# A two-layer hybrid decoder step with the order of every engine's steps written out as tables

## The chip, the cores and the metric

The kernel runs on one core of one Trainium2 chip. The metric is device time in microseconds (us), as the median of the runs. Six places matter: TensorE (PE), VectorE (DVE), ScalarE (ACT), GpSimd (POOL), SyncE (SP, which here only issues transfers), and the DMA engines that carry them out. Each engine works through its own list of instructions in order, and waits where an operand isn't ready.

## The reference

Two layers of one decoder block, over 1024 new tokens of a prompt and 8 × 4 tokens of running samples, in float32. The reference, cut to its core:

```python
def mixer_layer(x, pos, S0, k_past, v_past, buf, n_past, norm_pre, w_in, ret_gn_w, sb_bias, ...):
    h = rmsnorm(x, norm_pre)
    p = h @ w_in
    rq, rk, rv, rg, sq, sk, sv, sg, ca, cb, cg = jnp.split(p, idx, axis=-1)
    o_r, S = retention(rope(rq), rope(rk) * HEAD_DIM ** -0.5, rv, S0)
    o_r = head_groupnorm(o_r, ret_gn_w) * jax.nn.silu(rg)
    o_s = stickbreak(sq, k_all, v_all, sb_bias, n_past) * jax.nn.silu(sg)
    o_c, buf_new = conv_module(ca, cb, buf, dw_w, dw_b, ln_w, ln_b, pw_w)
    o_c = o_c * jax.nn.silu(cg)
    y = jnp.concatenate([o_r, o_s, o_c], axis=-1) @ w_out
    return x + rmsnorm(y, norm_post), S, sk_h, sv_h, buf_new
```

The model is 1024 wide, has 6 retention heads and 6 stick-breaking heads of 64, and a causal convolution over 31 tokens in 256 channels. In stick-breaking attention a score z gives log_stop = log sigmoid(−z), and its weight is exp(log sigmoid(z) + the sum of log_stop over all keys between it and the query), so every block of keys needs the totals of the blocks behind it.

## The kernel before

The 1056 tokens lie along the free axis, in 3 chunks of 352 (c = 0, 1, 2). What each engine does is cut into named **steps**, and each engine's program is a loop over a list of such steps that opens a branch for each kind. A step's instructions and its semaphore waits are the same wherever it stands in the list.

- **proj.i.c**: column block i of a weight matrix times chunk c. A layer has 54 blocks: 30 of the input projection, then 24 of the output projection, whose 8 column blocks come once for each chunk. A step has 24 matmuls of 128 rows × 352 columns. Each weight and each activation is split into a high and a low part, so eight row blocks take three products each: high·high (L1199), weight high · activation low (L1200), weight low · activation high (L1201). The result goes to one of three PSUM banks used in turn (`ring`). `claim` (L1171) makes PE wait until the bank's former job has been copied out by ACT (`proj` on ACT, L1611 among others).
- **wload.i** (L1447, a DMA issued by ACT), **whi.i** (ACT, L1459) and **wlo.i** (DVE or POOL, L1049) bring a block's weights in and split them.
- **sqx** (ACT, L1488), **sum_x** (PE, L1426), **nrm** (DVE, L1796), **hi** (ACT, L1580) and **lo** (L1040) make the normed, split activations of a chunk: squares, their sum, scaling, high and low part.
- Retention works on pairs of heads (p = 0 to 5, three in each layer). **swap** (SP, L1121) and **rot** rotate queries and keys, **glu_rest** (SP, L1087 and L1088) stores the convolution's state, **dec** (POOL, L2057 and L2061) applies the decay, **vtok** (PE, L1212) turns values over, **att.p.n** (PE, L1222 and L1224) and **ro.p.n** (PE, L1241, L1249, L1256) make block n of 128 tokens, and **gn_mean** (PE, L1278) and **gn_var** the group norm.
- Stick-breaking attention works on the same pairs, in 12 units u of a key block and a run of queries. Unit u goes through **score** (PE L1323, then ACT exp L1528, POOL L2101), **log** (ACT L1536, DVE L1770), **halve** (ACT L1550, DVE L1777), **stop** (PE L1337 and L1339, then ACT L1709) and **weigh** (PE totals L1353 and L1354, ACT L1719, PE product with the values L1359). `halve` of unit u on ACT waits for the totals of `weigh` of unit u − 1, which read the same buffers.
- The convolution (**taps** on DVE L1916, its norm **ln_mean** on PE L1290), and for the sample tokens **sample_k**, **sample_v** and **sample_o** on PE, with exp on ACT at L1743.
- The end of a layer: **root_y** (L1183), **post** (DVE L2042), **res** (L1031), and the stores of the result from SP: **store.l.c.h** (L1163), two for each chunk and four for the last chunk. **oldx** (SP, L1155) brings the residual back, **pages** (SP, L1059) copies 16 pages of the key or value cache.

Most matmuls use the whole array, 128 rows by 128 columns of weights. Some don't, and hold two or four small ones at a time: `score` 64 × 128, the value product of `weigh` 128 × 64, `ro` 64 × 64 and 128 × 64, `sum_x`, `sample_k` and `sample_v` 128 × 32. The profile prints this **form** beside the operation (as 64*128).

What sets the order is a planner, run when the kernel is built. `plan` (L532 to L706) names every step with a guessed duration and the steps that it needs; `RANKS` and `TURNS` hold numbers that push a kind of step, or one step, forward or back; `Plan.order` then replays the whole program: at each turn it picks, over all engines, the ready step with the lowest start time plus penalty. On PE it adds 0.09 where a step begins in another form than the last one ended. Five lists come out: 702 steps for PE, 1118 for ACT, 853 for DVE, 246 for POOL and 91 for SP.

Of the kernel before, what the change touches and what calls it, by code (L numbers as in the profile page):

```python
# [141 lines left out]
GATES = [("cb", 0), ("cb", 1), ("rg", 0), ("sg", 0), ("ln_act", 1), ("ln_act", 0), ("sg", 1), ("rg", 1), ("cg", 0), ("cg", 1), ("rg", 2), ("sg", 2)]  # L142
LATE = [("gn", 0), ("ln", 0), ("gn", 1), ("gn", 2)]
# [51 lines left out]
def helper(q):  # L195
# [3 lines left out]
SHARED_BY_DVE = ("taps", "taps9", "halve", "join", "rot", "gated", "wlo", "lo", "splo", "res", "glu_rest", "ln_act", "ln_var", "gn_var")  # L199
SHARED_BY_POOL = ("wlo", "rot", "dec", "own", "lo", "splo", "res")  # L200


RANKS = {("DVE", "log"): 2, ("PE", "ro"): -5, ("PE", "all_x"): -26, ("DVE", "sample_l"): 3, ("ACT", "root_x"): 2, ("SP",
         "glu_rest"): 296, ("SP", "pages"): 51, ("POOL", "res"): -11, ("DVE", "ln_act"): 12, ("SP", "oldx"): 239.5, ("SP",
         "swap"): 29.5, ("POOL", "own"): 9, ("SP", "store"): 147.5, ("ACT", "ln_act"): 6, ("SP", "stout"): 97, ("ACT", "gn_var"):
         2.5, ("PE", "sum_x"): -34, ("PE", "sample_o"): 21.5, ("DVE", "att"): 2.5, ("POOL", "rot"): 0.5, ("DVE", "halve"): 1,
         ("PE", "proj"): 4.5, ("POOL", "dec"): -3, ("PE", "vtok"): -42, ("DVE", "glu_rest"): 13.5, ("ACT", "wload"): 1, ("SP",
         "vout"): 125.5, ("PE", "weigh"): -4.5, ("POOL", "wlo"): 1, ("DVE", "post"): -9, ("DVE", "ln_var"): 1, ("PE", "stop"):
         -3.5, ("ACT", "att"): -7.5, ("PE", "att"): -5.5, ("DVE", "rot"): 2, ("ACT", "score"): 0.5, ("DVE", "q9"): 13, ("ACT",
         "proj"): 0.5, ("DVE", "taps"): 0.5, ("PE", "score"): 1.5, ("DVE", "res"): -8.5, ("ACT", "sample_l"): 2.5, ("DVE",  # L210
         "sample_o"): 6, ("ACT", "ro"): -7.5, ("PE", "gn_var"): 5, ("PE", "pw"): -51, ("ACT", "sigmoid"): -1, ("DVE", "st"): 0.5,
         ("POOL", "score"): -1.5, ("ACT", "halve"): 0.5, ("ACT", "pw"): -4.5, ("DVE", "ln_mean"): 1.5, ("SP", "pwload"): 212,
         ("ACT", "log"): -1, ("ACT", "k9"): 8, ("PE", "sample_v"): -76.5, ("DVE", "gn_mean"): 0.5, ("ACT", "root_y"): 1.5,
         ("ACT", "sample_k"): -1, ("ACT", "hi"): -2, ("ACT", "part"): 1, ("ACT", "gn_mean"): 1.5, ("ACT", "weigh"): -0.5, ("DVE",
         "wlo"): -0.5, ("DVE", "join"): 0.5, ("DVE", "proj"): 0.5}
# [59 lines left out]
class Plan:


    def __init__(self):
# [11 lines left out]
    def order(self):  # L290
# [18 lines left out]
        while left:  # L309
            best = None  # L310
            for n, t in ready.items():
                e, step = n
                if e == "PE" and step[0] in ring_kinds:
# [8 lines left out]
                    if t is None:  # L322
                        continue
# [1873 lines left out]
```

## Time and profile before

| | us |
|---|---|
| median of 3 runs | 1347.22 (1347.12 to 1348.54) |
| the profiled execution, span | 1346.0 |
| PE busy in it | 1317.3 (98%) |
| DVE busy | 834.3 (62%) |
| ACT busy | 772.9 (57%) |
| POOL busy | 464.9 (35%) |

The span is the time from the first to the last instruction of the profiled execution, which was one run of the same program as the timed ones. Matmuls of one stream overlap in the records: each is shown with 0.32 us and the next begins 0.16 us later. So the time that a stretch on PE costs is read from the starts of its rows, and not from their durations.

### The profile page before, as it was taken

What the parts mean: (1) busy time and instruction counts of PE and PEld (TensorE: products, weight loads), DVE (VectorE), ACT (ScalarE), POOL (GpSimd) and SP (SyncE); (2) the same over time, 40 slices, a digit from 0 to 9 for tenths busy, and PEclk for the clock granted to TensorE, in tenths of its full rate; (3) what the DMA queues carried; (4) which work ended last, traced back from release to release, by engine and by line L of the source; (5) the groups of instructions that cost most, each with busy time, mean ns of one, the idle gap of its engine ahead of it and who ended that gap; (6) DMA issues with size and microseconds to landing.
All of it is one profiled execution on the core that took longest, in us unless ns stands there. A gap on an engine that the chain in (4) does not pass through costs nothing.

```text
span 1346.0 us, 23077 instructions
## 1 busy us (share of the span) xinstructions
PE 1317.3 (98%) x8532; PEld 1136.4 (84%) x8532; DVE 834.3 (62%) x1306; ACT 772.9 (57%) x1535; POOL 464.9 (35%) x418
## 2 busy tenths in 40 slices
PE   6999999999999999999999999999999999999996
PEld 4988788887788887899998888888879788789996
DVE  4447787986542446466773587889764245554665
ACT  6464554655564666575655555456575456667552
POOL 2424532344422444141243345324343423423111
PEclk9999999999999999999999999999999999999998
DMA  7301103212024100275343120131101321006453
GB/s 251 113 22 57 38 32 91 81 46 60 17 69 132 56 19 30 73 237 171 109 139 123 43 57 32 57 113 44 47 26 54 80 83 48 33 10 226 154 184 118
DMA packets 92242, 113.61 MB, mean 84 GB/s; under 512 B 30818, under 2 KB 75618, under 8 KB 92002
## 3 DMA queue, kind: packets, MB, share of 16 engines
q1 hardware_dynamic: 76866, 56.56, 14.0%
q10 hardware_dynamic: 15264, 55.58, 12.8%
q8 instruction: 68, 1.11, 0.4%
q14 instruction: 44, 0.36, 0.1%
HBM read 88.15 MB, written 17.46 MB: 78 GB/s over the span
## 4 chain that ended last, share of the span: by engine, by line
PE 94%; ACT 2%; DVE 1%; POOL 1%; issue 1%; DMA 0%; SPq 0%; ACTq 0%; DVEq 0%; POOLq 0%
PE ring L1199 23%; PE ring L1201 21%; PE ring L1200 21%; PE Z L1323 4%; PE AV L1359 4%; PE Z L1337 2%; PE Z L1339 2%; PE ring L1278 2%; PE ring L1222 2%; PE Z L1353 2%; PE Z L1354 1%; PE ring L1241 1%; PE ring L1301 1%; PE ring L1237 1%; PE ring L1290 1%
## 5 line engine op out<-in xcount | busy, mean ns | idle before, releaser
L1199 PE MATMUL ring<-H_hi,w_hi 128*128 128x352 f32 x1776 | 594.3, 335 | 5.7 <-DVE H_lo L1040 4.9
L1201 PE MATMUL ring<-H_hi,w_lo 128*128 128x352 f32 x1776 | 572.3, 322 | 0.0
L1200 PE MATMUL ring<-H_lo,w_hi 128*128 128x352 f32 x1776 | 571.1, 322 | 0.0
L1199 PEld LDWEIGHTS ring<-H_hi,w_hi 128*128 128x128 f32 x1776 | 334.1, 188 | 43.2 <-issue 30.8
L1200 PEld LDWEIGHTS ring<-H_lo,w_hi 128*128 128x128 f32 x1776 | 335.1, 189 | 4.5
L1201 PEld LDWEIGHTS ring<-H_hi,w_lo 128*128 128x128 f32 x1776 | 334.4, 188 | 0.0
L2101 POOL TENSOR_SCALAR attend<-attend 128x512 f32<-128x512 f32 (+4 forms) x144 | 188.9, 1328 | 319.4 <-ACT attend L1528 319.3
L1916 DVE SCALAR_TENSOR_TENSOR MX<-MX,vec_sb 128x1023 f32<-128x1023 f32 (+14 forms) x120 | 166.7, 1389 | 2.2
L1770 DVE SCALAR_TENSOR_TENSOR attend<-Z,vec_sb,attend 128x512 f32<-128x512 f32 (+4 forms) x144 | 85.4, 612 | 86.7 <-ACT attend L1536 86.3
L1459 ACT ACTIVATE w_hi<-w_raw 128x1024 fp32r<-128x1024 f32 x80 | 84.6, 1057 | 64.7 <-PE ring L1201 36.2
L1536 ACT ACTIVATE attend<-attend 128x512 f32<-128x512 f32 (+4 forms) x144 | 73.6, 524 | 64.7 <-POOL attend L2101 64.3
L1049 DVE TENSOR_TENSOR w_lo<-w_raw,w_hi 128x1024 fp32r<-128x1024 f32 x52 | 66.8, 1285 | 66.0 <-ACT w_hi L1459 65.9
L1049 POOL TENSOR_TENSOR w_lo<-w_raw,w_hi 128x1024 fp32r<-128x1024 f32 x28 | 67.7, 2418 | 82.3 <-ACT w_hi L1459 82.3
L1528 ACT ACTIVATE attend<-Z,vec_sb 128x512 f32<-128x512 f32 (+4 forms) x144 | 75.5, 582 | 24.0 <-PE Z L1329 17.2
L1777 DVE TENSOR_TENSOR stop_lo<-attend,stop_hi 128x512 fp32r<-128x512 f32 (+4 forms) x144 | 82.0, 609 | 10.5 <-ACT stop_hi L1550 10.2
L1709 ACT ACTIVATE attend<-Z,vec_sb 128x512 f32<-128x512 f32 (+4 forms) x144 | 75.6, 579 | 14.0 <-PE Z L1339 13.6
L2057 POOL TENSOR_TENSOR qd<-ret_q,decay_sb 128x256 f32<-128x256 f32 (+1 forms) x54 | 39.5, 731 | 121.3 <-PE ring L1241 106.4
L1550 ACT ACTIVATE stop_hi<-attend 128x512 fp32r<-128x512 f32 (+4 forms) x144 | 68.5, 521 | 5.0 <-DVE attend L1770 3.9
L1623 ACT ACTIVATE gate<-ring 128x352 f32<-128x352 f32 x54 | 25.1, 464 | 79.1 <-PE ring L1201 78.9
L2009 DVE TENSOR_TENSOR MX<-MX,keep 128x384 f32<-128x384 f32 (+5 forms) x60 | 42.3, 704 | 38.6 <-PE AV L1359 33.8
L1323 PE MATMUL Z<-sb_q,sb_k 64*128 64x512 f32 (+5 forms) x288 | 65.4, 533 | 0.0
L1359 PE MATMUL AV<-attend 128*64 128x512 f32 (+5 forms) x288 | 62.3, 511 | 0.3 <-ACT attend L1650 0.3
(184 smaller groups left out, 1845.0 us busy)
## 6 DMA issues: line engine op xcount, KB each, us to landing
w_raw<-in_w ACTq DMA_DIRECT2D x81, 512.0 KB, 3.5
state<-in_w ACTq DMA_DIRECT2D x25, 512.0 KB, 3.6
out_yT<-MX SPq DMA_DIRECT2D x10, 704.0 KB, 5.0
swapped<-raw_rot SPq DMA_DIRECT2D x144, 44.0 KB, 1.9
attend<-in_cache_k SPq DMA_DIRECT2D x96, 64.0 KB, 1.9
attend<-in_cache_v SPq DMA_DIRECT2D x96, 64.0 KB, 2.1
attend<-in_xT SPq DMA_DIRECT2D x3, 1408.0 KB, 10.8
attend<-out_yT SPq DMA_DIRECT2D x3, 1408.0 KB, 11.1
```

The source lines that it names most:

```text
L1049: ops.tensor_tensor(wide_lo[slot(i)], raw_of(i), wide_hi[slot(i)].bitcast(F32), ALU.subtract).then_inc(sg.sem, sg.mark(i))
L1199: nc.tensor.matmul(in_ring(step), a, x, start=(n_k == 0), stop=False)
L1200: nc.tensor.matmul(in_ring(step), a, y, start=False, stop=False)
L1201: last = nc.tensor.matmul(in_ring(step), b, x, start=False, stop=(n_k == KB - 1))
L1323: last = nc.tensor.matmul(Z[2 * (u % 2) + h][:, 0:n], sb_k[r, kb * P:(kb + 1) * P], sb_q[r, q0:q0 + n], start=True, stop=not diagonal, ski ...
L1359: last = nc.tensor.matmul(AV[64 * h:64 * h + 64, 0:n], sb_v[:, kb, 64 * h:64 * h + 64], stop_of(u, h), start=True, stop=True, skip_group_c ...
L1459: nc.scalar.activation(wide_hi[slot(i)], raw_of(i), ACT.Copy).then_inc(s_whi.sem, s_whi.mark(i))
L1709: nc.scalar.activation(stop_of(u, h), Z[2 * (u % 2) + h][:, 0:n], ACT.Exp, bias=vv(p // PAIRS, V_BIAS + 2 * (p % PAIRS) + h)).then_inc(s_a ...
L1770: nc.vector.scalar_tensor_tensor(out=s, in0=Z[2 * (u % 2) + h][:, 0:n], scalar=vv(p // PAIRS, V_BIAS + 2 * (p % PAIRS) + h), in1=s, op0=AL ...
L1777: nc.vector.tensor_tensor(stop_lo[:, h, 0:n], stop_of(u, h), stop_hi[:, h, 0:n].bitcast(F32), ALU.subtract).then_inc(s_splo.sem, s_splo.ma ...
L1916: nc.vector.scalar_tensor_tensor(out=y, in0=glu[b][:, 0:SEQ - s], scalar=w, in1=y, op0=ALU.mult, op1=ALU.add).then_inc(s_tap.sem, s_tap.ma ...
L2101: nc.gpsimd.tensor_scalar(s, s, E_MAX, None, ALU.min).then_inc(s_min.sem, s_min.mark((p, u, h)))
```

## The change

The planner with its numbers (`RANKS`, `TURNS`, `Plan`, `plan`, `keep_order`) is taken out. In its place stand five literal lists of step names, one for each engine, and `orders` reads them. The lists hold the same steps as before, 702, 1118, 853, 246 and 91 of them, in another order. The branches that write out a step's instructions and its waits are the same, 251 lines further up (L1199 is L948 now), and so are the buffers. At 330 of its 702 positions PE has the same step as before, ACT at 153 of 1118, DVE at 117 of 853, POOL at 123 of 246 and SP at 16 of 91; most steps stand a few places away from where they were.

```diff
-def orders():
-
-    return plan().order()
+TABLES = {
+    "PE": """
+sum_x.0.0.0 sum_x.0.0.1 all_x.0.0 proj.0.0 sum_x.0.1.0 sum_x.0.1.1 proj.1.0 all_x.0.1 sum_x.0.2.0 sum_x.0.2.1 proj.2.0
...
+    return {engine: [step_of(text) for text in table.split()] for engine, table in TABLES.items()}
...
-                    act.wait_ge(s_full.sem, s_full.at(last_proj(user_before(i))[1]))
+                    act.wait_ge(s_full.sem, s_full.at(last_proj(user_before(i))))
```

Four places show what moves.

**PE, pair 2, units of 448 and 384 queries.** `Z` holds scores, totals and stops, `AV` the products with the values, `ring` the projection. Before, the weights of one unit stood alone between projection steps:

```order
L1353 MATMUL Z<-stop_hi,neg_r 128x448
L1354 MATMUL Z<-stop_lo,neg_r 128x448
L1353 MATMUL Z<-stop_hi,neg_r 128x448
L1354 MATMUL Z<-stop_lo,neg_r 128x448
L1359 MATMUL AV<-attend 64x448 x2
L1199 MATMUL ring<-H_hi,w_hi 128x352
L1200 MATMUL ring<-H_lo,w_hi 128x352
L1201 MATMUL ring<-H_hi,w_lo 128x352
```

```order
L1102 MATMUL Z<-stop_hi,neg_r 128x448
L1103 MATMUL Z<-stop_lo,neg_r 128x448
L1102 MATMUL Z<-stop_hi,neg_r 128x448
L1103 MATMUL Z<-stop_lo,neg_r 128x448
L1108 MATMUL AV<-attend 64x448 x2
L1072 MATMUL Z<-sb_q,sb_k 128x384 x2
L948 MATMUL ring<-H_hi,w_hi 128x352
L949 MATMUL ring<-H_lo,w_hi 128x352
L950 MATMUL ring<-H_hi,w_lo 128x352
```

The scores of a later unit (L1072) now follow the value product directly, and the projection comes after both.

**PE, the first two retention blocks of pair 0.** Before, att.0.0 and att.0.1 followed each other, behind the last projection step of block 8's first chunk:

```order
L1201 MATMUL ring<-H_hi,w_lo 128x352
L1222 MATMUL ring<-qd,kd 128x256
L1224 MATMUL ring<-const,kd 128x128
L1222 MATMUL ring<-qd,kd 128x256
L1224 MATMUL ring<-const,kd 128x128
L1353 MATMUL Z<-stop_hi,neg_r 128x320
```

```order
L961 MATMUL ring<-const,attend 128x128 x6
L971 MATMUL ring<-qd,kd 128x256
L973 MATMUL ring<-const,kd 128x128
L948 MATMUL ring<-H_hi,w_hi 128x352
L949 MATMUL ring<-H_lo,w_hi 128x352
L950 MATMUL ring<-H_hi,w_lo 128x352
...
L961 MATMUL ring<-const,attend 128x128 x3
L971 MATMUL ring<-qd,kd 128x256
L973 MATMUL ring<-const,kd 128x128
```

Now the projection step (24 matmuls) and a part of `vtok` stand between the two.

**SP, the end of the program.** Before, the three loads of the residual came first, then two stores of chunk 1 and four of chunk 2:

```order
L1155 DMA attend<-out_yT 128x8x352 x3
L1163 DMA out_yT<-MX 128x4x352 x4
L1163 DMA out_yT<-MX 128x2x352 x4
```

```order
L904 DMA attend<-out_yT 128x8x352 x2
L912 DMA out_yT<-MX 128x4x352
L904 DMA attend<-out_yT 128x8x352
L912 DMA out_yT<-MX 128x4x352 x2
L912 DMA out_yT<-MX 128x2x352 x2
L912 DMA out_yT<-MX 128x4x352
L912 DMA out_yT<-MX 128x2x352 x2
```

One half of chunk 1 (128x4x352, store.1.1.0) now stands between the first two and the last two stores of chunk 2.

**ACT, the first squares, splits and weights of the program.** Before, the load of weight block 2 stood behind the first four high parts of chunk 0, and all squares behind the other four:

```order
L1580 ACTIVATE H_hi<-wide 128x352 x4
L1447 DMA w_raw<-in_w 128x1024
L1580 ACTIVATE H_hi<-wide 128x352 x2
L1488 ACTIVATE raw_rot<-MX 128x352 x2
L1580 ACTIVATE H_hi<-wide 128x352 x2
L1488 ACTIVATE swapped<-MX 128x352 x2
```

```order
L1329 ACTIVATE H_hi<-wide 128x352 x4
L1237 ACTIVATE raw_rot<-MX 128x352 x2
L1237 ACTIVATE swapped<-MX 128x352 x2
L1329 ACTIVATE H_hi<-wide 128x352 x4
L1196 DMA w_raw<-in_w 128x1024
L1237 ACTIVATE gate<-MX 128x352 x2
L1208 ACTIVATE w_hi<-state 128x1024
```

Four squares of chunk 1 (into `raw_rot` and `swapped`) now stand ahead of the second four high parts, and the load behind them. On SP, in the same way, the store of the convolution's state glu_rest.0 moved from behind the swaps of pair 0's keys to between the first chunk's swaps and the second's, and some of the groups of 16 page copies, which stood between blocks, now stand between two chunks' swaps.

## Rows read from the trace of the kernel before

**Rows 1.** The page: span, busy time, and the chain by engine

```profile
span 1346.0 us, 23077 instructions
PE 1317.3 (98%) x8532; PEld 1136.4 (84%) x8532; DVE 834.3 (62%) x1306; ACT 772.9 (57%) x1535; POOL 464.9 (35%) x418
PE 94%; ACT 2%; DVE 1%; POOL 1%; issue 1%; DMA 0%; SPq 0%; ACTq 0%; DVEq 0%; POOLq 0%
```

**Rows 2.** Windows: stretch, then busy (count) by engine, PE clock, DMA share, GB/s

```profile
200.00:300.00 100.00, 100.00 (x667) 84.48 (x666) 85.21 (x110) 55.95 (x112) 35.70 (x22) 1.00 0.24 70
```

**Rows 3.** Timeline of PE at 233 us: start, us, engine, line, operation, count [idle]

```profile
233.12 0.32 PE L1200 MATMUL ring<-H_lo,w_hi 128*128 128x352 f32 x1
233.28 0.32 PE L1201 MATMUL ring<-H_hi,w_lo 128*128 128x352 f32 x1
233.53 1.13 PE L1323 MATMUL Z<-sb_q,sb_k 64*128 64x512 f32 x4
234.59 0.43 PE L1199 MATMUL ring<-H_hi,w_hi 128*128 128x352 f32 x1
234.86 0.32 PE L1200 MATMUL ring<-H_lo,w_hi 128*128 128x352 f32 x1
```

**Rows 4.** Timeline of PE at 434 and 444 us

```profile
434.25 0.55 PE L1212 MATMUL ring<-const,attend 128*128 128x128 f32 x3 [0.53 <-DVE MX L1837]
434.73 1.08 PE L1359 MATMUL AV<-attend 128*64 128x512 f32 x4
435.74 0.43 PE L1199 MATMUL ring<-H_hi,w_hi 128*128 128x352 f32 x1
...
444.52 1.08 PE L1359 MATMUL AV<-attend 128*64 128x512 f32 x4
445.53 0.65 PE L1323 MATMUL Z<-sb_q,sb_k 64*128 64x448 f32 x2
```

**Rows 5.** Timeline of PE at waits between 148 and 860 us

```profile
148.57 0.67 PE L1222 MATMUL ring<-qd,kd 128*128 128x256 f32 x2 [1.14 <-POOL kd L2061]
...
331.84 0.67 PE L1222 MATMUL ring<-qd,kd 128*128 128x256 f32 x2 [0.36 <-POOL kd L2061]
...
377.47 0.86 PE L1278 MATMUL ring<-MX,const 128*128 128x352 f32 x2 [0.66 <-ACT sb_k L1611]
...
550.42 0.81 PE L1278 MATMUL ring<-MX,const 128*128 128x352 f32 x2
551.35 0.30 PE L1353 MATMUL Z<-stop_hi,neg_r 128*128 128x128 f32 x1
...
859.77 0.28 PE L1224 MATMUL ring<-const,kd 128*128 128x128 f32 x1
860.11 0.30 PE L1353 MATMUL Z<-stop_hi,neg_r 128*128 128x128 f32 x1
```

**Rows 6.** Timeline of POOL ahead of 148.57 us

```profile
139.82 1.13 POOL L2074 TENSOR_TENSOR swapped<-swapped,turn_sb 128x352 f32<-128x352 f32 x1 [4.14 <-DMA swapped<-raw_rot]
```

**Rows 7.** Timeline of ACT at 18 us, and of PE at 25 us

```profile
18.45 0.99 ACT L1580 ACTIVATE H_hi<-wide 128x352 fp32r<-128x352 f32 x2 [1.79 <-DVE wide L1796]
...
25.57 0.43 PE L1199 MATMUL ring<-H_hi,w_hi 128*128 128x352 f32 x1 [0.58 <-DVE w_lo L1049]
```

**Rows 8.** SP's queue in the tail, and one window of the last us (columns as in 2)

```profile
1339.52 3.83 SPq L1163 DMA_DIRECT2D out_yT<-MX  x4
...
1344.00:1345.00 1.00, 0.00 (x0) 0.00 (x0) 0.00 (x0) 0.00 (x0) 0.00 (x0) 0.50 1.05 390
```

**Rows 9.** Timeline of PE at 1153 us (stop.5.6), and of ACT at 220 us

```profile
1153.12 0.39 PE L1337 MATMUL Z<-stop_hi,negtri_r 128*128 128x320 f32 x1
1153.88 0.41 PE L1339 MATMUL Z<-stop_lo,negtri_r 128*128 128x320 f32 x1 [0.37 <-DVE stop_lo L1777]
...
220.47 0.57 ACT L1743 ACTIVATE stop<-Z,vec_sb 128x96 f32<-128x96 f32 x2 [0.25 <-PE Z L1397]
```

**Rows 10.** Timeline of SP's queue at 32 us: 16 page copies

```profile
32.54 8.54 SPq L1059 DMA_DIRECT2D attend<-in_cache_k  x16
```

More of the change, by code:

```diff
@@ L196, in helper @@
     return "POOL" if q in (1, 2) else "DVE"
[L199 to L215, printed above, removed]
@@ L372, in keep_order @@
-def keep_order(g):
-    last = {}
-    for node in list(g.nodes):
-        e, step = node
-        if step[0] in ("score", "log", "att", "dec", "st", "own", "rot", "swap", "vtok", "wload", "whi", "wlo"):
-            line = (e, step[0])
-        elif step[0] == "proj":
-            line = (e, "out") if LOAD[step[1]][0] == "out" else (e, "turn") if LOAD[step[1]][0] in ("rq", "rk") and e == "ACT" else (e, step[0], step[1])
-        else:
-            continue
-        if line in last:
-            g.nodes[node][1].append((last[line], -5.0))
-        last[line] = node
@@ new lines @@
+proj.19.1 ln_act.0 weigh.1.11 whi.21 proj.19.2 gn_mean.1.0 sample_k.1 gn_mean.1.1 sample_z.1 gn_var.1.0 score.2.0 sample_l.1
+proj.20.0 pw.0.0 log.2.0 proj.20.1 halve.2.0 sample_t.1 pw.0.1 sample_v.1 wload.22 pw.0.2 whi.22 wload.23 proj.20.2 proj.21.0
+proj.21.1 proj.21.2 stop.2.0 whi.23 score.2.1 wload.24 gn_var.1.1 vtok.sv.2.0 log.2.1 proj.22.0 score.2.2 halve.2.1 log.2.2
+proj.22.1 stop.2.1 vtok.sv.2.1 halve.2.2 proj.22.2 whi.24 score.2.3 stop.2.2 log.2.3 proj.23.0 proj.23.1 weigh.2.2 wload.25
@@ new lines @@
+halve.2.9 att.2.6 wload.28 weigh.2.8 proj.27.0 whi.28 ro.2.6 att.2.7 stop.2.9 att.2.8 ro.2.7 weigh.2.9 score.2.10 log.2.10
+ro.2.8 halve.2.10 score.2.11 log.2.11 proj.27.1 stop.2.10 gn_mean.2.0 halve.2.11 gn_mean.2.1 weigh.2.10 gn_mean.2.2 stop.2.11
+gn_var.2.0 proj.27.2 weigh.2.11 sigmoid.cg.1 gn_var.2.1 sample_k.2 sample_z.2 wload.29 sample_l.2 proj.28.0 proj.28.1 whi.29
+sample_t.2 gn_var.2.2 proj.28.2 wload.30 sample_v.2 sigmoid.rg.2 proj.29.0 split.0.0.2 wload.31 whi.30 split.0.0.1 split.0.0.0
@@ new lines @@
+score.5.11 gn_mean.5.0 log.5.11 whi.82 gn_mean.5.1 halve.5.11 weigh.5.10 proj.81.1 stop.5.11 gn_var.5.0 gn_mean.5.2 proj.81.2
+weigh.5.11 sigmoid.cg.3 sample_k.5 wload.83 gn_var.5.1 sample_z.5 sample_l.5 proj.82.0 sample_t.5 gn_var.5.2 whi.83 proj.82.1
+proj.82.2 wload.84 sample_v.5 sigmoid.rg.5 split.1.0.2 split.1.0.0 whi.84 split.1.0.1 proj.83.0 split.1.0.3 proj.83.1 wload.85
+wload.86 whi.85 whi.86 proj.83.2 split.1.1.1 proj.84.0 wload.87 whi.87 split.1.1.0 proj.85.0 split.1.2.1 wload.88 proj.86.0
@@ L715, in build, with step_of, orders @@
+""",
+}
+def step_of(text):
+    name, *rest = text.split(".")
+    return (name, *(int(x) if x.isdigit() else x for x in rest))
+def orders():
+    return {engine: [step_of(text) for text in table.split()] for engine, table in TABLES.items()}
+def last_proj(i):
+    return ("proj", i, LOAD[i][1][1] if LOAD[i][0] == "out" else CH - 1)
 def build(nc, io, counts):
```

668 lines of the change are left out of this document (231 added, 437 removed).

## The prediction, made before the change was run

> **What bounds the kernel now.** I read the page first: PE is busy in 1317.3 of 1346.0 us, the other engines in 62% or less, and PE is 94% of the chain that ended last [rows 1]. Then the windows, for the question whether that busy time is work: between 200 and 300 us PE has no idle time at all and its clock is 1.00, while DVE, the next engine, has 85 [rows 2]. The windows between 100 and 1333 us all look like it. So PE is the bound, and since the change keeps every matmul, only four things can move the time: what stands between two matmuls of one stream without being a wait, the few waits in the middle, the head before PE's stream is fed, and the tail after the last projection step. For these I went to the timeline, and read the starts of the rows, because the durations of matmuls overlap.
>
> An engine that is off the path counts here only where it makes PE wait, or where the new order brings it closer to doing so. I take the change in those five parts.
>
> **A. Form changes on PE.** In one stream, matmuls of 352 columns begin 0.16 us apart (233.12 to 233.28). The first `score` matmul begins 0.25 after the last projection matmul, 0.09 more. When the stream comes back, 234.59 to 234.86 is 0.27, 0.11 more [rows 3]. So a visit to a small form, in and out, costs 0.20. A change from one small form to another seems to cost no more than the way out does: the four `AV` matmuls take 1.01 to the next start, whether a projection step follows (434.73 to 435.74) or a `score` in its other form (444.52 to 445.53) [rows 4].
>
> I counted both orders on PE. `weigh` is followed directly by a `score` 27 times where it was 13 times, and by a projection step 8 times where it was 24, as the first place of the change shows. Entries from the full array into a small form fall from 165 to 136, all changes of form from 427 to 392. So 29 visits go: 29 × 0.20 = **−5.8**. Lower bound of the gain: if only the way in is saved, since the change between two small forms has a price of its own, 29 × 0.09 = 2.6. Upper bound: the group itself may be stretched too. Four matmuls of 512 columns at the stream's rate of 352 in 0.16 would take 0.93, and the `score` group takes 1.06 (233.53 to 234.59), so a visit would be 0.09 + 0.13 + 0.11 = 0.33, and A 29 × 0.33 = 9.6. I take 5.8 because both halves of the visit are read from rows, and the time of a change between small forms from its own row.
>
> The Trainium skill, "TensorEngine Tiling (Array Packing)", Key Properties, says that changing the tiling mode drains TensorE. If a drain meant that all overlap of neighbours was lost, each of the two changes would cost the 0.32 of a record less the 0.16 between starts, and term A would be 29 × 0.32 = 9.3; the rows show 0.09 and 0.11, so by the trace the drain is a partial one, and the sum keeps 5.8.
>
> **B. Waits in the middle that the new order fills.** The largest is at 148.57: PE stands 1.14 for POOL's `kd` [rows 5], since POOL itself waited 4.14 for a swap to land [rows 6]. In the new order a projection step (24 matmuls, 24 × 0.16 = 3.9 us of work) stands between att.0.0 and att.0.1, as the second place shows. That is more than the wait, so it goes whole. The same is so of the waits at 331.84 (0.36), 377.47 (0.66) [rows 5] and 434.25 (0.53) [rows 4]: a projection step or another unit's work now lies in front of each. Three shorter ones have no idle time printed, but the starts show them: 550.42 to 551.35 is 0.93, some 0.5 more than the two matmuls need, and 859.77 to 860.11 is 0.34 for one matmul of 128 columns, some 0.3 too long, as at one more place just before it [rows 5]. Together 1.14 + 0.36 + 0.66 + 0.53 + 0.5 + 0.3 + 0.3 = 3.8: **−3.8**. Next late after each is PE's own next step, so no engine stands behind it. The bound below is half of it (−1.9), if what fills a place was cover for another wait.
>
> **C. The head.** ACT has nothing to do for 1.79 us until 18.45, as it waits for the scaled activations, and PE waits 0.58 at 25.57 for the low part of block 1's weights [rows 7]. The new order puts four squares of chunk 1 into that hole. They must be done anyway before `whi` of block 1, which reaches the split on DVE that PE waits for: the hole is larger than PE's wait. So **−0.6**, bounds −0.6 and 0. Moved with them is the load of weight block 2, which is issued behind four squares and four more high parts now; its matmuls come behind two more steps of PE, which cover that.
>
> **D. The tail.** The four stores of the last chunk are issued between 1339.52 and 1343.35, and from 1344 to 1345 the DMA engines are full: share 1.05, 390 GB/s [rows 8]. So the end of the program is the end of that traffic. The third place of the change puts half of chunk 1's result, 128 × 4 × 352 × 4 bytes = 704 KB, between the second and the third store of chunk 2; before, it was issued ahead of them all. 721 thousand bytes at 390 GB/s are 1.85 us. **+1.9**. Bounds: 0, if the DMA engines have room for it between 1338 and 1342, and +2.9, if the issue also holds SP for one store (3.83 / 4 = 0.96 [rows 8]).
>
> The Trainium skill, "DMA: Bandwidth & Descriptors", Queues, rings and completion order, says that each DMA engine takes the descriptors of a queue in ring order; by that rule the last two stores stand behind all of the 704 KB even if they are small, and the trace can't show it, as before had nothing large there.
>
> **E. New tight places.** Where order fills one place it opens another. `halve` of a unit waits for the totals of the unit before it, and `stop` on PE for `halve`. In the new order stop.3.2, stop.5.3 and stop.5.8 stand 1.3 to 1.4 us of PE work behind the totals, where it was 3.9 to 6.9 (the instructions between the two in either order, at the intervals of the trace). The nearest row is stop.5.6, which had 1.0: its second matmul begins 0.76 after the first, where 0.15 would do [rows 9], so a wait of 0.6. Three of them: 1.8. Twice (pairs 0 and 3) the step between the samples' turn and sample_v is now `ds9` alone, 0.5 us, against an exp on ACT of 0.57 for two with its waits [rows 9]: 2 × 0.25 = 0.5. **+2.3**; bounds 0 and 4.6, as the 702 steps may hold as many again that I didn't find.
>
> **The sum.** −5.8 − 3.8 − 0.6 + 1.9 + 2.3 = −6.0. The profiled execution took 1346.0 and would take 1340.0; the median of the runs stands 1.2 above its span, and I keep that distance: 1347.2 − 6.0 = **1341.2**.
>
> **The rivals.**
> 1. *The waits only move.* DVE is at 85% in places [rows 2], so nothing is far from late. For it: the tight places that I found are already worth 2.3 and have no row of their own. Against: PE's gain in A doesn't depend on waits, and in the stretches with 100% busy there were none. With eleven waits of 0.6 instead of three and a bit, E is 6.6: 1347.2 − 5.8 − 3.8 − 0.6 + 1.9 + 6.6 = 1345.5.
> 2. *The form price isn't there.* The ends of matmuls are modelled, and a start 0.09 late may be made up by the rest of the stream. For it: no wait is printed at such a place. Against: the row behind it begins late too, and the sum over a whole visit is what I counted. Then A = 0, and B to E give −0.2: 1347.0.
> 3. *Slower: a page group between the swaps of one block.* 16 page copies hold SP for 8.54 us [rows 10]. They now stand between two chunks' swaps at pairs 1, 4 and 5. The later swap is 8.5 us late, its rotation with it, and behind that the copy of a `ring` bank into `raw_rot` by ACT, for which `claim` stops PE. It decides when the block's next use of `raw_rot` or `att` of that pair has less than 8.5 us of PE work before it; by the order there are some 30. If two places lose the whole of it: 1341.2 + 17 = 1358; if one, 1349.7.
> 4. *Better.* The tail's store finds room (D = 0) and the tight places don't wait (E = 0.4): 1347.2 − 5.8 − 3.8 − 0.6 + 0.4 = 1337.4.
>
> That the change doesn't do what it says can be left aside: the lists hold the same steps with the same waits, and the order is seen in them.
>
> **How the numbers follow.** My forecast 0.60, rival 1 0.12, rival 2 0.08, rival 3 0.07, rival 4 0.13. The predicted time is the first's, 1341.2. The range: A at 9.6 with D and E of rival 4 would be 1333.6, and I stop at 1335.5, since all three together are unlikely; A at 2.6 with E at its bound of 4.6 is 1346.7, and I stop at 1346.5. Rival 2 and rival 3 stay outside (0.15). A difference of 0.2%, 2.7 us, is what can be told from none. Of the forecast's chance, 0.55 lies below 1344.5 and 0.05 above. Rival 1 is 0.11 same and 0.01 faster; rival 2 is 0.06 same and 0.01 to either side; rival 3 is 0.06 slower and 0.01 same; rival 4 is faster. So faster 0.55 + 0.01 + 0.01 + 0.13 = 0.70, same 0.05 + 0.11 + 0.06 + 0.01 = 0.23, slower 0.07.
>
> **What would show it.** A: at the places where `score` follows `AV`, the `AV` group takes 1.01 to the next start, and PE's busy time falls by 4 to 6 us, while the idle time falls less. B: no wait over 0.3 at att.0.1, att.1.1, gn_mean.1.1. C: ACT idle under 0.5 before 18.5, and the second block's first matmul without a wait. D: two windows or more at 380 to 390 GB/s at the end, and a stretch from the last projection matmul to the end about 1.9 longer than before. E: waits of 0.6 at stop.3.2, stop.5.3, stop.5.8. I would be wrong if PE's busy time doesn't fall, if `rot` waits for a swap behind a page group, or if DVE has new waits for PE in its full stretches that come back to PE as late `stop_lo`.

## The result: slower, and the profile after

The changed kernel took 1353.6 us (median of 4 runs, 1352.7 to 1354.7) against 1347.2 for the kernel before. The ratio is 1.0043, 95% interval 1.0031 to 1.0056. The prediction was 1341.2 with a range to 1346.5 and a chance of 0.07 for slower: it was wrong in size and in sign.

The page of the profile after, first lines (span, then busy us by engine), to be read against [rows 1]:

```profile
span 1352.7 us, 23077 instructions
PE 1314.1 (97%) x8532; PEld 1138.8 (84%) x8532; DVE 827.2 (61%) x1306; ACT 765.4 (57%) x1535; POOL 466.6 (34%) x418
```

PE's busy time did fall, by 3.2 us, and the span grew by 6.7. So the loss isn't more work on PE: most of it is time in which PE waits, and some is time in which its clock is low, as shown below. The waits of PE, first of after (the row is: engine, line, waited for whom, us in total, times, longest):

```profile
PE ring L948 <- DVE H_lo L789: 6.1, 3, 4.9
PE Z L1175 <- ACT raw_rot L1237: 4.5, 1, 4.5
PE AV L932 <- DVE sb_k L1601: 2.9, 1, 2.9
PE ring L948 <- DVE w_lo L798: 2.3, 2, 1.4
PE Z L1158 <- ACT stop L1492: 2.2, 1, 2.2
PE Z L932 <- DVE sb_k L1601: 2.1, 2, 1.5
PE Z L1102 <- DVE MX L1760: 1.6, 1, 1.6
PE ring L948 <- ACT raw_rot L1341: 0.9, 1, 0.9
```

then of before:

```profile
PE ring L1199 <- DVE H_lo L1040: 4.9, 1, 4.9
PE Z L1426 <- ACT raw_rot L1488: 4.5, 1, 4.5
PE ring L1222 <- POOL kd L2061: 1.5, 2, 1.1
```

The first two rows of each are the head, which is the same (of the 6.1 it is the longest wait, 4.9). Below them before has small waits only, and after has waits on five different producers. Only one of them is named by a term of the prediction, the exponential ahead of `sample_v`, and that at 0.25. They look unrelated. Most of them have one cause, which shows on ACT and not on PE. ACT's longest waits for a transfer of weights, after:

```profile
ACT w_hi L1208 <- DMA w_raw<-in_w: 48.2, 24, 4.6
ACT w_hi L1208 <- DMA state<-in_w: 26.4, 16, 3.4
```

and before:

```profile
ACT w_hi L1459 <- DMA w_raw<-in_w: 28.5, 12, 5.8
```

For `state` it was 2.2 us in 3 waits before.

ACT issues the load of a weight block (`wload`) and splits the block later (`whi`). Between the two there was, for the blocks of the input projection (without the first two loads of the head), a median of 13.4 us before and of 6.5 after, from the start of the issue to the start of the split in both traces; under 5 us it was 7 of 56 times before and 18 of 56 after. A block of 512 KB takes about 3.5 us from issue to landing (median in both traces). So in the new order ACT often issues a load, does next to nothing, and stands in front of the split. One such place, ACT from 220.9 us, after:

```profile
220.92 0.46 ACT L1360 ACTIVATE sb_k<-ring 128x352 f32<-128x352 f32 x1 [1.74 <-PE ring L950]
220.92 0.33 ACTq L1196 DMA_DIRECT2D w_raw<-in_w  x1
224.37 1.06 ACT L1208 ACTIVATE w_hi<-w_raw 128x1024 fp32r<-128x1024 f32 x1 [2.99 <-DMA w_raw<-in_w]
225.34 0.55 ACT L1492 ACTIVATE stop<-Z,vec_sb 128x96 f32<-128x96 f32 x2
```

and what PE did meanwhile:

```profile
223.19 0.59 PE L1015 MATMUL ring<-wide,kd_tok 128*64 128x512 f32 x1
225.94 0.43 PE L1158 MATMUL Z<-own_v,stop 128*32 128x128 f32 x8 [2.15 <-ACT stop L1492]
```

The exponential at 225.34 (sample_t.0) had its input when PE had finished sample_t at 222.8. It stood behind a split that waited 2.99 us for a load issued at 220.92, and PE waited 2.15 us for the exponential. The row on PE names ACT's exponential, which is true and hides the load two steps further back.

The wait has a second cost, on PE's own clock. Its granted clock was 1.00 from 22 us on, and fell to 0.50 (1.2 of 2.4 GHz) from 226.96 to 230.37 us, just behind that wait. Here are two windows of after (columns as in [rows 2]), then one group of four matmuls, first in after and then in loads_four, a run below in which PE has no such wait there:

```profile
227.00:230.00 3.00, 3.00 (x27) 1.11 (x15) 0.00 (x0) 0.38 (x1) 1.96 (x1) 0.50 0.00 0
231.00:234.00 3.00, 3.00 (x21) 3.00 (x21) 2.93 (x3) 2.03 (x5) 2.93 (x2) 1.00 0.00 0
...
227.75 2.08 PE L1072 MATMUL Z<-sb_q,sb_k 64*128 64x512 f32 x4
...
223.18 1.13 PE L1072 MATMUL Z<-sb_q,sb_k 64*128 64x512 f32 x4
```

The same happens once more in after, from 653.62 to 657.04 us, behind the wait of 2.92 us that ends at 652.24: the projection matmuls begin 0.29 apart there, where 0.16 is usual. In before the clock is 1.00 from 22 us until PE's work is done. No wait is printed for the time that this costs.

To add up PE's whole time I priced each stretch of it (one matmul, or a group of equal small ones) by what the same stretch between the same neighbours takes elsewhere (the lower quartile over all traces of this case, where there are three places or more), and took the rest as waiting, or, where the granted clock was 0.50, as its price:

| us | before | after |
|---|---|---|
| start of the second stretch | 11.4 | 11.2 |
| stretches at their price | 1298.1 | 1289.9 |
| over the price, up to 40 us | 9.1 | 8.6 |
| waits over 0.3, after 40 us | 7.5 | 18.3 |
| over the price at a granted clock of 0.50 | 0.0 | 3.2 |
| smaller remainders | 9.3 | 9.0 |
| start of the last matmul | 1335.4 | 1340.2 |
| from there to the end | 10.6 | 12.5 |

The loss is in three rows: long waits, 10.8 more, the low clock behind two of them, 3.2, and the tail, 1.9. The gain is in the second row.

### The profile page after: what moved, and what is told of

Same layout as the page of the kernel before. It is cut to its first block and busy times, and to the rows that moved or that the text cites. A ratio compares the mean times of both kernels' runs of the same rounds, so it can differ in the third digit from the quotient of the medians.

```text
span 1352.7 us, 23077 instructions
## 1 busy us (share of the span) xinstructions
PE 1314.1 (97%) x8532; PEld 1138.8 (84%) x8532; DVE 827.2 (61%) x1306; ACT 765.4 (57%) x1535; POOL 466.6 (34%) x418
## 5 line engine op out<-in xcount | busy, mean ns | idle before, releaser
L948 PE MATMUL ring<-H_hi,w_hi 128*128 128x352 f32 x1776 | 590.7, 333 | 10.0 <-DVE H_lo L789 6.1
L948 PEld LDWEIGHTS ring<-H_hi,w_hi 128*128 128x128 f32 x1776 | 334.7, 188 | 36.0 <-issue 25.3
L1665 DVE SCALAR_TENSOR_TENSOR MX<-MX,vec_sb 128x1017 f32<-128x1017 f32 (+27 forms) x120 | 162.8, 1364 | 1.3
L798 POOL TENSOR_TENSOR w_lo<-w_raw,w_hi 128x1024 fp32r<-128x1024 f32 x28 | 72.3, 2584 | 80.9 <-ACT w_hi L1208 80.9
L1072 PE MATMUL Z<-sb_q,sb_k 64*128 64x512 f32 (+5 forms) x288 | 66.1, 539 | 0.0
L1823 POOL TENSOR_TENSOR swapped<-swapped,turn_sb 128x352 f32<-128x352 f32 x36 | 38.5, 1071 | 70.4 <-DMA swapped<-raw_rot 70.4
L780 POOL TENSOR_TENSOR MX<-MX,attend 128x352 f32<-128x352 f32 x24 | 26.2, 1120 | 95.8 <-DVE MX L1791 95.6
```

What stands on the lines that cost most here:

```text
L798: ops.tensor_tensor(wide_lo[slot(i)], raw_of(i), wide_hi[slot(i)].bitcast(F32), ALU.subtract).then_inc(sg.sem, sg.mark(i))
L948: nc.tensor.matmul(in_ring(step), a, x, start=(n_k == 0), stop=False)
L1072: last = nc.tensor.matmul(Z[2 * (u % 2) + h][:, 0:n], sb_k[r, kb * P:(kb + 1) * P], sb_q[r, q0:q0 + n], start=True, stop=not diagonal, ski ...
L1665: nc.vector.scalar_tensor_tensor(out=y, in0=glu[b][:, 0:SEQ - s], scalar=w, in1=y, op0=ALU.mult, op1=ALU.add).then_inc(s_tap.sem, s_tap.ma ...
```

## The experiments

Theory 1: the loads stand too close to their splits, ACT works in order, and what stands behind the split reaches PE late. Theory 2, the nearest to what the prediction had feared: the order of PE and DVE leaves too little work between dependent steps, whatever the loads do. Diffs are in the names of steps; all times are medians, and the kernel before, measured beside each, stood at 1346.5 to 1346.9 (1347.2 beside after). Each trace is one execution.

### All loads earlier: loads_early

On ACT each `wload` moves up to the first place at which, by the trace of after, its buffer was free. Nothing else changes. For block 9 and block 62 this reads:

```diff
-... log.0.6 ... whi.8 proj.7.2 score.0.7 ... att.0.3 ro.0.1 wload.9 whi.9
+... log.0.6 ... whi.8 proj.7.2 wload.9 score.0.7 ... att.0.3 ro.0.1 whi.9
...
-score.3.6 halve.3.5 proj.60.1 stop.3.5 log.3.6 proj.60.2 weigh.3.5 halve.3.6 wload.62 whi.62
+score.3.6 halve.3.5 wload.62 proj.60.1 stop.3.5 log.3.6 proj.60.2 weigh.3.5 halve.3.6 whi.62
```

> The changed kernel, with each load of a weight block on ACT moved up to the earliest place at which, by its trace, the block it overwrites had been split already (up to 20 steps up, up to 23 us earlier); nothing else. Theory 1 (the loads stand so close to the split that uses them that ACT, which works in order, stops for the transfer, and what stands behind the split on ACT reaches PE late): the waits of PE at 166.4, 225.9, 652.2, 806.4, 952.8, 1241.8, 1251.2 and 1322.7 us, 12.6 us together, mostly go, and the time falls by 6 to 10 us from the changed kernel's 1353.6, to 1344 to 1348. Theory 2 (the new order of DVE and PE has too little work between dependent steps, whatever the loads do): at most 2 us less, 1351.6 or more.

Measured: 1343.8, ratio to before 0.9975 (0.9965 to 0.9985). That is 9.8 us less than after, and less than before. PE's waits in it, without the head:

```profile
PE AV L932 <- DVE sb_k L1601: 2.7, 1, 2.7
PE Z L932 <- DVE sb_k L1601: 1.5, 1, 1.5
PE ring L948 <- DVE w_lo L798: 1.3, 1, 1.3
```

The waits on the exponential, on `MX`, on `raw_rot` and one of the two on `w_lo` are gone; those in the turn between the layers (the first row) and in the last output projection stayed, which theory 1 as I had written it expected to go too: of the 12.6 us that it named some 6 went. That the time fell by the full 6 to 10 us is partly luck, since the stretch at a granted clock of 0.50 behind the wait on the exponential went with it (1.5 us). Median lead of the loads: 11.9 us. Theory 2 fails for the most part: the same order of PE, DVE, POOL and SP, with other leads, is the faster kernel.

### Four loads only: loads_four

> The changed kernel, with only four loads moved up on ACT, those of weight blocks 9, 13, 62 and 70, by 20, 5, 6 and 9 steps. Theory 1: exactly the waits of PE at 166.4 (1.05), 225.9 (2.22), 806.4 (1.74) and 952.8 us (1.06) go, 6.1 us together, and the waits in the turn between the layers and in the last output projection stay: 1347.5 to 1349. Theory 2: the four waits stay or shrink by less than half, 1351 or more.

Measured: 1345.9, 0.9989 (0.9980 to 0.9998), 7.7 us less than after, by moving four transfers; its eleven runs spread from 1341.3 to 1348.0. In its trace the four waits are gone; the one of root_y.0.1 stayed (3.5 for 2.9), and so did those of the last output projection. It went 1.6 us beyond the sum of the four waits. In the trace that is what the stretch at a granted clock of 0.50 right behind sample_v.0 had cost: the same matmuls take 1.6 us less there, with the clock at 1.00. Two short waits of 0.4, at stop.3.5 and att.3.0, went too, and root_y.0.1 took most of them back. So the fall of the clock hangs on the wait ahead of it; the other one, behind root_y.0.1, stayed with its wait.

### The same place from the other side: split13_later

If the fault is the place in ACT's line, it must also go when the load stays late and only the split steps aside:

```diff
-... proj.11.2 wload.13 whi.13 sample_t.0 sample_v.0
+... proj.11.2 wload.13 sample_t.0 whi.13 sample_v.0
```

> The changed kernel, with the split of weight block 13 moved on ACT from ahead of the exponential sample_t.0 to behind it; its load stays where it was, late. If the loss at 225.9 us is one of place in ACT's line (the exponential is ready, but stands behind an instruction that waits for a transfer), PE's wait of 2.2 us there goes though the load is as late as before: 1351.0 to 1351.6 against 1353.6. If the exponential was late for another reason, nothing changes.

Measured: 1351.7, 1.0043 (1.0029 to 1.0057) of the before measured beside it, 1.9 us less than after. ACT in that place:

```profile
218.75 0.33 ACTq L1196 DMA_DIRECT2D w_raw<-in_w  x1
220.64 0.57 ACT L1492 ACTIVATE stop<-Z,vec_sb 128x96 f32<-128x96 f32 x2 [1.44 <-PE Z L1146]
222.33 1.06 ACT L1208 ACTIVATE w_hi<-w_raw 128x1024 fp32r<-128x1024 f32 x1 [1.12 <-DMA w_raw<-in_w]
```

The load has a lead of 3.6 us as before and lands as late, the exponential no longer stands behind it, and PE has no wait over 0.3 there, nor a fall of its clock. So this late transfer costs nothing by itself; what costs is the ready work queued behind it. Two cautions: three new waits of 0.4 came up within the next 40 us, so the 1.9 is a net figure; and the runs of the two kernels overlap (1351.1 to 1354.2 against 1352.7 to 1354.7), so it is the trace that shows this and not the 1.9.

### The cause put into the kernel before: before_late

Ten loads of the old order moved down to directly ahead of their own splits, as `wload.9 ... whi.9` to `... wload.9 whi.9`.

> The kernel before, with ten loads (weight blocks 9, 13, 22, 27, 29, 61, 69, 72, 78, 79) moved down on ACT to directly ahead of their own split; nothing else. Theory 1: ACT stops about 3.5 us at each, as long as a transfer takes, and where a copy or an exponential that PE soon needs stands behind it PE waits 1 to 2 us: 2 to 8 us slower than before. Theory 2: the order before has cover enough, and the time stays within 1 us.

Measured: 1359.3, 1.0094 (1.0079 to 1.0108), 12.4 us slower, half more than the upper end expected. One of the places, ACT and then PE:

```profile
558.50 1.06 ACT L1208 ACTIVATE w_hi<-w_raw 128x1024 fp32r<-128x1024 f32 x1 [3.57 <-DMA w_raw<-in_w]
559.46 0.26 ACT L1468 ACTIVATE keep<-Z 128x128 f32<-128x128 f32 x1
...
559.82 0.66 PE L1118 MATMUL Z<-q_pad,wide 128*128 128x64 f32 x2 [2.96 <-issue]
```

What PE needs next there (the copy into `keep`) stands behind the split. The view names no releaser ("issue"), but sample_k waits in the kernel for that copy, and PE begins 0.1 us after it ends. Of the 11.7 us by which PE's last matmul came later, 8.6 are waits over 0.3, some 3 are a stretch at a granted clock of 0.50 from 559.55 to 566.38 us, behind the wait shown, and 1 is smaller waits. I had left the clock out. The run is the strongest evidence for theory 1, since it makes a slower kernel out of the faster one by this one thing.

### Early loads in the old order: before_early

> The kernel before, with each load of a weight block on ACT moved up by the same rule, from its own trace (44 loads can move, by 0.1 to 10 us, since most stand there already). Theory 1: ACT's waits for these transfers, 28 us in 12 places, shrink little and stand where PE has cover, so the gain is small, 0 to 1.5 us. If early loads are worth as much in any order (a rival to the reading that the changed order lost what the order before had), it gains 5 us or more.

Measured: 1347.4, 1.0000 (0.9991 to 1.0009). No gain. Earlier loads are worth nothing in the old order, so loads_early's gain is the repair of a loss that the new tables brought, and not a general one.

### The tail: store_first

```diff
-oldx.1.1 store.1.1.1 store.1.0.0 store.1.2.1 store.1.2.2 store.1.1.0 store.1.2.3 store.1.2.0
+oldx.1.1 store.1.1.1 store.1.1.0 store.1.0.0 store.1.2.1 store.1.2.2 store.1.2.3 store.1.2.0
```

> The changed kernel, with the store of the second chunk's first half (704 KB) moved back on SP from between the second and third store of the last chunk to right behind the second chunk's other half. If the tail grew by 1.9 us because the last stores queue behind these 704 KB, the time falls by 1.9 and the stretch from the last root_y matmul to the end falls from 12.5 to 10.6. If the tail grew for another reason, nothing changes (within 0.5).

Measured: 1351.7, 1.0040 (1.0027 to 1.0052), 1.9 us less than after. The six runs spread from 1350.9 to 1356.4, so the medians alone wouldn't show it; the trace does: from the last matmul's start to the end it is 10.6 us as before, where after had 12.5. (The profiled execution was one of 1355.2: both stretches at a granted clock of 0.50 last 6.8 us in it, where after had 3.4.) After, the last windows (columns as in [rows 2]) show the extra traffic; in [rows 8] the last full window ends at 1345:

```profile
1348.00:1350.00 2.00, 0.00 (x0) 0.00 (x0) 0.00 (x0) 0.00 (x0) 0.00 (x0) 0.50 1.05 388
1350.00:1352.00 2.00, 0.00 (x0) 0.00 (x0) 0.00 (x0) 0.00 (x0) 0.00 (x0) 0.50 0.91 334
```

The rule quoted in the prediction (the Trainium skill, "DMA: Bandwidth & Descriptors", Queues, rings and completion order: a DMA engine takes a queue's descriptors in ring order) can now be held against a run: the last stores paid the full 704 KB ahead of them, 1.9 us at 388 GB/s, which agrees with it.

### The price of a form change: forms_apart

From loads_early, 22 scores on PE move from directly behind a value product to behind the projection step that follows:

```diff
-weigh.0.3 score.0.5 proj.6.1
+weigh.0.3 proj.6.1 score.0.5
```

> The kernel loads_early with 22 of its scores moved on PE from directly behind a value product to behind the projection step that follows: 22 more entries from the full array into a small form, and 22 more changes of form in all. If a visit costs 0.20 (the prediction's price), the intervals of PE's stream without waits add up to 4.4 more; if each change costs 0.09 whatever the two forms, to 2.0 more. The whole time grows by that and by what the later scores (4 us each) cost in new waits, which the trace shows apart.

Measured: 1386.3, 1.0292 (1.0275 to 1.0309), 42.5 us slower than loads_early. The stretches at their price grew from 1289.9 to 1294.2, by 4.3: so 22 × 0.20, the price of a visit. One of the 22 places, first in loads_early and then in forms_apart, without any wait:

```profile
436.61 1.08 PE L1108 MATMUL AV<-attend 128*64 128x512 f32 x4
...
442.50 0.37 PE L1086 MATMUL Z<-stop_hi,negtri_r 128*128 128x448 f32 x1
442.70 0.36 PE L1088 MATMUL Z<-stop_lo,negtri_r 128*128 128x448 f32 x1
...
443.30 0.32 PE L948 MATMUL ring<-H_hi,w_hi 128*128 128x352 f32 x1
```

```profile
447.33 1.08 PE L1108 MATMUL AV<-attend 128*64 128x512 f32 x4
...
452.35 1.02 PE L1072 MATMUL Z<-sb_q,sb_k 64*128 64x448 f32 x4
453.31 0.47 PE L1086 MATMUL Z<-stop_hi,negtri_r 128*128 128x448 f32 x1
453.62 0.36 PE L1088 MATMUL Z<-stop_lo,negtri_r 128*128 128x448 f32 x1
...
454.23 0.33 PE L948 MATMUL ring<-H_hi,w_hi 128*128 128x352 f32 x1
```

From the first row to the last it is 6.69 us in the one and 6.90 in the other, for the same matmuls. The way in costs 0.09 (as in [rows 3]; here the projection matmul ahead of 452.35 begins at 452.10) and the way back 0.11 (453.31 to 453.62 is 0.31, and 442.50 to 442.70 is 0.20). Of the other 38 us some 26 are waits over 0.3, and 9 are six stretches at a granted clock of 0.50, where loads_early has one. They are the greater lesson. The longest of the new rows in PE's list:

```profile
PE Z L1086 <- ACT stop_hi L1299: 9.9, 6, 2.3
```

A score 4 us later makes the exponential, the minimum on POOL, the log, the halves and the stop of its unit 4 us later. With `weigh` of the same unit at its old place there was no room for that; ACT stood 5 us for the scores at 274.6 and then did everything in one go:

```profile
274.56 0.58 ACT L1277 ACTIVATE attend<-Z,vec_sb 128x384 f32<-128x384 f32 x1 [5.03 <-PE Z L1078]
```

So the adjacency of score and weigh that the new order brought is worth 0.20 a place as a saved visit. What it is worth as an early score this run doesn't say, since here the rest of the order had been made for the early one.

### Repairs: tuned, tuned2, tuned3

tuned is loads_early with the store of store_first and four single steps moved:

```diff
 PE:   -root_y.0.1 proj.47.2                      +proj.47.2 root_y.0.1
 DVE:  -proj.83.0 splo.1.0.3 splo.1.0.0           +splo.1.0.0 proj.83.0 splo.1.0.3
 DVE:  -wlo.85 proj.83.2 proj.84.0 wlo.86         +wlo.85 wlo.86 proj.83.2 proj.84.0
 ACT:  -whi.104 whi.105 wload.106 proj.101.2      +proj.101.2 whi.104 whi.105 wload.106
```

> The kernel loads_early with five places put right by its trace: store.1.1.0 ahead of the last chunk's stores (1.9), root_y.0.1 behind proj.47.2 on PE (2.8 to 3.8), on DVE splo.1.0.0 ahead of proj.83.0 (1.0) and wlo.86 right behind wlo.85 (1.5), on ACT proj.101.2 ahead of whi.104 (1.0). If each of these waits belongs to the one step that stands ahead of what is waited for, they go without a new one: 1343.8 - 8.5 = 1335.3. If they move on to the next step, most of it comes back and only the 1.9 of the tail is sure: 1341.9.

Measured: 1341.2, 0.9960 (0.9947 to 0.9974). The tail gave its 1.9, the four moves together nearly nothing. In the trace the waits had moved: 1.0 and 1.5 at 1232 and 1242 became one of 2.7, and the 2.8 at root_y.0.1 became 1.5, 1.7 and 1.2 in the next 25 us. The stretch at a granted clock of 0.50 moved with them: from behind root_y.0.1 to 1237.46, behind the wait of 2.7. Its row:

```profile
1237.30 0.49 PE L948 MATMUL ring<-H_hi,w_hi 128*128 128x352 f32 x1 [2.56 <-DVE w_lo L798]
```

I had put right the last step of each chain and not its first. Block 85's split waited for its load, which stood directly ahead of it; the rule of loads_early had skipped it, because that load waits for a store and not for a split. tuned2 moves it up, with block 86's, and ten others by the new trace:

```diff
-split.1.0.2 split.1.0.0 whi.84 split.1.0.1 proj.83.0 split.1.0.3 proj.83.1 wload.85 wload.86 whi.85 whi.86
+split.1.0.2 split.1.0.0 whi.84 wload.85 split.1.0.1 proj.83.0 wload.86 split.1.0.3 proj.83.1 whi.85 whi.86
```

> The kernel tuned, with ten loads moved up once more by its own trace (1 to 3 steps), and the loads of weight blocks 85 and 86, which stood directly ahead of their splits, moved up to behind the split of block 84 and ahead of the last split of chunk 0. If the wait of 2.7 us at 1237.3 in tuned, which took the place of two others, comes from these loads, it goes whole and the time is 1338.0 to 1338.8. If ACT and DVE are simply full in that stretch, the wait moves on and the time stays at 1340.5 to 1341.5.

Measured: 1338.7, 0.9941 (0.9927 to 0.9954): 2.5 less. The wait of 2.7 is gone whole and none took its place, and the stretch at 0.50 behind it is gone too, so that the traces differ there by 4.3; why the medians differ by less is open. That left the turn between the layers, where ACT in tuned2 read (first the load's issue):

```profile
627.74 0.33 ACTq L1196 DMA_DIRECT2D w_raw<-in_w  x1
632.00 1.06 ACT L1208 ACTIVATE w_hi<-w_raw 128x1024 fp32r<-128x1024 f32 x1 [4.61 <-DMA w_raw<-in_w]
```

A ready copy (proj.42.1, on PE done at 624.6) and the next load, issued at 632.01, both stood behind that split. tuned3:

```diff
-whi.45 wload.46 whi.46 wload.47 part.1.0 proj.42.1
+whi.45 wload.46 proj.42.1 wload.47 whi.46 part.1.0
...
-wload.52 whi.51 sqx.1.1.0 whi.52 wload.53 whi.53 wload.54 hi.1.0.2 hi.1.0.3 wload.55 proj.49.2 part.1.1
+whi.51 wload.52 sqx.1.1.0 whi.52 wload.53 proj.49.2 part.1.1 whi.53 wload.54 hi.1.0.2 hi.1.0.3 wload.55
```

> The kernel tuned2, with five steps moved on ACT in the turn between the layers, where its PE still waits 1.4 (at 643.4), 1.7 (657.3) and 1.8 us (668.3): proj.42.1 and the load of block 47 ahead of the split of block 46, which waits 4.6 us for its own load; the load of block 52 behind the split of block 51; proj.49.2 and part.1.1 ahead of the split of block 53. If the three waits are again places in ACT's line behind something not ready, 3 to 4.5 us go: 1334.2 to 1335.7 against 1338.7. If ACT and DVE are full in the turn, they move on, and the time stays above 1337.5.

Measured: 1334.7, 0.9916 (0.9903 to 0.9930): 4.0 less again. Of the three waits named two went (at 643.4 and 668.3 in tuned2), and the one on `w_lo` at 657.3 stayed (1.6 for 1.7). The same stretch of ACT now, with the load issued before the split is waited for and the copy done in the gap:

```profile
627.32 0.33 ACTq L1196 DMA_DIRECT2D w_raw<-in_w  x1
627.70 0.46 ACT L1375 ACTIVATE MX<-ring 128x352 f32<-128x352 f32 x1 [0.72 <-DVE w_lo L798]
628.89 0.33 ACTq L1196 DMA_DIRECT2D state<-in_w  x1
631.39 1.06 ACT L1208 ACTIVATE w_hi<-w_raw 128x1024 fp32r<-128x1024 f32 x1 [2.88 <-DMA w_raw<-in_w]
```

tuned3 beats both kernels: 11.8 us under before, 18.9 under after, with PE busy in 98% of its span and no stretch at a granted clock of 0.50 between the head and the tail:

```profile
PE 1307.5 (98%) x8532; PEld 1136.5 (85%) x8532; DVE 834.3 (63%) x1306; ACT 767.0 (58%) x1535; POOL 469.9 (35%) x418
```

## Why the prediction was wrong, term by term

**Form changes (A), −5.8 predicted, −5.8 by the rows.** Right. The two prices hold where forms_apart moves a visit by itself (0.09 in and 0.11 back, 22 of them 4.3 us), and so does the reading that a change between two small forms has no price beyond the way out. In the whole orders entries from the full array fall by 29 and returns to it by 29, and 29 × 0.20 is 5.8. The stretches at their price fell by 8.2, more than that: at least 1.0 of the rest is waits of before at places that no other place matches (0.7 at 377.47, 0.3 at 860.11), so that they were priced as work, and 1.4 I can't place. PE's busy time fell by 3.2 where 4 to 6 were forecast, because the matmuls at a granted clock of 0.50 are in it with 3.2 us more.

**Waits that the new order fills (B), −3.8 predicted.** Right, and a little small: the waits at 148.57, 331.84, 377.47, 434.25, 551.35 and around 859 us [rows 4, 5] are gone in after, and that in stop.5.6 [rows 9] with them, some 5 us together. The gain was real and was outweighed.

**The head (C), −0.6 predicted.** The wait is gone as said: the second block's stream begins at 25.10 without a wait, where it began at 25.57 with one of 0.58 [rows 7], and ACT's hole before 18.34 shrank to 0.25:

```profile
18.34 1.97 ACT L1329 ACTIVATE H_hi<-wide 128x352 fp32r<-128x352 f32 x4 [0.25 <-DVE wide L1545]
```

What it was worth in time is not shown: the first projection matmul begins at 17.8 in after and at 15.6 in split13_later and store_first, which have the same head, so that one execution differs from the next by more than the 0.6.

**The tail (D), +1.9 predicted, +1.9 measured**, and store_first took it away again.

**New tight places (E), +2.3 predicted with an upper bound of 4.6.** This is the step that failed. New long waits are some 15 us against the 5 that went, and two of them brought 3.2 us at a granted clock of 0.50, for which the sum had no term, so E was about 18. Both halves of the term were off. The three places that it named for 0.6 each have no such wait: behind stop.3.2 the second matmul begins 0.29 after the first,

```profile
766.64 0.45 PE L1086 MATMUL Z<-stop_hi,negtri_r 128*128 128x448 f32 x1
766.93 0.37 PE L1088 MATMUL Z<-stop_lo,negtri_r 128*128 128x448 f32 x1
```

and stop.5.3 and stop.5.8 have at most 0.27. The fourth, sample_v of pair 0, was named for 0.25 and cost 2.2, by another mechanism: not the short `ds9` between, but the load ahead of the split ahead of the exponential. The bound rested on one measure, how much PE work lies between two dependent steps. It left out what stands between them in the line of the engine in the middle. In the prediction the load's place came up once, for block 2 in the head, and there it was judged only by whether the block comes in time for PE. The question "what is queued behind the split while it waits" was asked for no load. The material was there: in the lists of ACT `wload` stands directly ahead of its `whi` 15 times in the new tables, where it did so 3 times.

**The rivals.** Rival 3 (page copies between swaps) was the one that ended slower, and it didn't reach PE: POOL's waits for the swaps grew from 41.6 us in 10 to 70.4 in 23, but the one wait on `kd` that PE's list shows in after is 0.2 us. Rival 1 (waits only move) was nearest in kind, with a size of 6.6 where some 18 was needed and 1345.5 as its time. Rival 2 (no price for the form) is refuted by forms_apart. None of them had a transfer issued by the engine that needs it as its mechanism. The statement that it "can be left aside" that the change doesn't do what it says looked only at whether the lists hold the same steps.

What stays open: in tuned3 four of PE's new waits are left, 3.1 us together, the longest of them on `w_lo` at 655.4, and no run traces them to a load. Why the clock fell behind some waits and not behind others isn't shown either: in after it did so behind 2.15 and 2.92 us and not behind the 1.58 at 806.41.

## What to carry to other kernels

On an engine that works in order, a transfer's lead is a property of its list: count for each load the time between its issue and its first use, compare it with issue to landing (3.5 us for 512 KB here), and where it is shorter ask what ready work stands behind the waiting instruction. When a wait on the bounding engine names a producer, follow the producer's own line back to its first idle time before you repair anything; moving the last step of the chain only moved the wait here, and moving the first one took it away. And a reordering is judged on every engine at once: bounds from the distance between dependent steps on the busiest engine alone were too small by more than a factor of three. When you add up waits, look at PE's granted clock behind the long ones as well: the matmuls there took 1.5 us or more longer, and no row of waits says so.

## What the runs showed of the hardware

- A visit to a small form costs 0.20 us on PE at a granted clock of 1.00, 0.09 on the way in and 0.11 on the way back, and going straight on into another small form saves it (4.3 us for 22 visits). The Trainium skill, "TensorEngine Tiling (Array Packing)", Key Properties, says that a change of mode drains the engine; the runs agree that there is a price, and both ways together it is a little over the 0.16 between two matmuls of 352 columns.
- Behind a plain f32 matmul of 352 columns the second projection matmul begins 0.43 after the first, where 0.16 is usual (652.67 to 653.10 in after). That is no price of the change: the first one is recorded 0.03 after the plain one, and the two together, 0.46, are what a plain one (0.30 to the next) and a projection matmul (0.16) take by themselves.
- Behind a long wait PE's granted clock was 0.50 for 3.4 us (6.8 in before_late and store_first), and the matmuls in such a stretch took 1.5 to 3 us more than at 1.00. Taking the wait away took the stretch away (loads_four at 227 us, tuned2 at 1237), and before_late put one into the order of before, which had none.
- Ten stops of ACT, of 1.2 to 4.8 us each and 30.7 together, on an engine that is busy in 57% of the span, cost the whole kernel 12.4 us, some 3 of them by PE's clock: an engine with 43% idle time had no slack to give away at the places where it waits.
